# MLA and pooling encoder with a 32-expert layer: slot table from one-hot products on chip, and the held part of the weight stream changed

## What is computed

```
h = x + concat(attention(rms_norm(x)), pooling(rms_norm(x))) @ w_out
y = h + HierMoE(rms_norm(h, g_ffn))
HierMoE(a): gp = softmax(a @ w_group_router + b_group_router)     # 4 groups, the best one
            el = a @ w_expert_router + b_expert_router            # 8 experts per group, the best two
            y  = sum over the two experts of gate * (silu(a @ w_gate[e]) * (a @ w_up[e])) @ w_down[e]
```

## Time and profile before

| what | value |
|---|---|
| median of three runs | 644.66 us |
| profiled execution, its own time | 643.67 us |
| its span, first to last instruction | 642.0 us |
| TensorE busy | 530.8 us (83%) |
| VectorE / ScalarE / GpSimd busy | 223.6 / 147.0 / 133.2 us |
| mean DMA rate | 232 GB/s |

### The profile page before, as it was taken

How to read it: one execution, slowest core, us unless ns; L and a number is a source line. 1 busy time by engine, 2 the same in 40 slices (tenths; PEclk the granted TensorE clock), 3 DMA queues, 4 the chain that set the end, 5 groups by cost and what they waited for, 6 DMA issues and landing times.

```text
span 642.0 us, 8839 instructions
## 1 busy us (share of the span) xinstructions
PE 530.8 (83%) x3092; PEld 373.3 (58%) x3093; DVE 223.6 (35%) x602; ACT 147.0 (23%) x310; POOL 133.2 (21%) x200
## 2 busy tenths in 40 slices
PE   5889999997898989999725877989788897777762
PEld 4768988884444568888624545555445564434430
DVE  4743335225959562566650211121211211111110
ACT  6734343322546221121201101010100100000000
POOL 0122232032244000034323102111201232011110
PEclk9999999999999999999856989799989999889997
DMA  8730100000620039243467999999999999999992
GB/s 333 240 142 35 32 2 1 1 0 1 236 72 27 2 137 387 100 132 133 171 227 253 405 374 388 392 367 379 388 393 390 392 392 379 403 390 392 388 363 34
DMA packets 31163, 148.81 MB, mean 232 GB/s; under 512 B 7139, under 2 KB 7798, under 8 KB 18822
## 3 DMA queue, kind: packets, MB, share of 16 engines
q1 hardware_dynamic: 25376, 128.60, 50.2%
q0 software_dynamic: 5712, 19.72, 11.7%
q10 hardware_dynamic: 38, 0.01, 0.0%
HBM read 132.48 MB, written 17.00 MB: 233 GB/s over the span
## 4 chain that ended last, share of the span: by engine, by line
DMA 45%; PE 25%; issue 10%; DVE 6%; POOL 4%; ACT 1%; POOLq 0%; SPq 0%
DMA expert_w<-in_w_down 25%; DMA expert_w<-in_w_up 19%; PE ps L476 4%; PE ps L477 4%; PE ps L481 4%; PE ps L641 3%; POOL slot_tokens L1390 2%; PE ps L582 2%; DVE p_sb L1130 2%; PE ps L596 2%; PE ps L599 1%; PE ps L628 1%; PE ps L516 1%; DMA g_rows<-token_rows,idx_now 1%; PE ps L667 1%
## 5 line engine op out<-in xcount | busy, mean ns | idle before, releaser
L767 PE MATMUL ps<-expert_w,xT 128*64 128x256 f32 x1152 | 132.2, 386 | 16.4 <-DMA expert_w<-in_w_up 6.8
L767 PEld LDWEIGHTS ps<-expert_w,xT 128*64 128x64 f32 x1152 | 97.7, 140 | 55.5 <-issue 27.8
L783 PE MATMUL ps<-expert_w,hT 128*64 128x512 f32 x288 | 76.8, 681 | 23.7 <-DMA expert_w<-in_w_down 13.2
L1432 POOL DMA_INDIRECT out<-y_sb,idx_now x18 | 28.7, 1593 | 202.6 <-DVE y_sb L1302 201.8
L783 PEld LDWEIGHTS ps<-expert_w,hT 128*64 128x64 f32 x288 | 25.5, 155 | 63.1 <-issue 60.7
L1290 DVE SCALAR_TENSOR_TENSOR hid<-s_act,gate,ps 128x256 f32<-128x256 f32 x18 | 11.9, 660 | 141.5 <-ACT s_act L968 141.5
L476 PE MATMUL ps<-w_in_hi,aT_hi 128*128 128x384 f32 (+2 forms) x120 | 43.7, 368 | 0.0
L1302 DVE COPY y_sb<-ps 128x512 f32<-128x512 f32 x18 | 12.5, 692 | 89.5 <-PE ps L783 89.5
L477 PE MATMUL ps<-w_in_lo,aT_hi 128*128 128x384 f32 (+2 forms) x120 | 40.8, 344 | 0.0
L968 ACT ACTIVATE s_act<-ps 128x256 f32<-128x256 f32 x18 | 6.9, 384 | 133.7 <-PE ps L767 133.7
L973 ACT ACTIVATE y_sb<-ps 128x512 f32<-128x512 f32 x18 | 10.8, 597 | 105.6 <-PE ps L783 105.6
(11 more groups left out here) (205 smaller groups left out, 856.5 us busy)
## 6 DMA issues: line engine op xcount, KB each, us to landing
expert_w<-in_w_gate SPq DMA_DIRECT2D x32, 1024.0 KB, 9.7
expert_w<-in_w_up SPq DMA_DIRECT2D x32, 1024.0 KB, 8.5
expert_w<-in_w_down SPq DMA_DIRECT2D x32, 1024.0 KB, 10.4
w_in_raw<-in_w_in SPq DMA_DIRECT2D x8, 608.0 KB, 10.3
w_out_raw<-in_w_out SPq DMA_DIRECT2D x8, 512.0 KB, 3.6
token_rows<-rows SPq DMA_DIRECT2D x6, 528.0 KB, 3.4
out<-h_sb SPq DMA_DIRECT2D x6, 512.0 KB, 2.9
x_sb<-in_x_prompt SPq DMA_DIRECT2D x4, 512.0 KB, 9.9
```

Of the source, the lines that this page charges most:

```text
L767: mm = pe.matmul(ps[r, 2, g * FH:(g + 1) * FH], xT[:, q.o, k, r], w_gu(b, lane, k, g), start=(k == 0), stop=(k == KD - 1))
L783: mm = pe.matmul(ps[r, 4 + half, :], hT[:, q.o, k, r], w_dn(b, lane, k, half), start=(k == 0), stop=(k == 1))
L1432: pool.indirect_dma_start(out=out, out_offset=bass.IndirectOffsetOnAxis(ap=idx, axis=0), in_=y_sb[:, buf, :], in_offset=None, compute_op=A ...
```

## The change

The slot table of the first pass is no longer read back from HBM. VectorE compares the place of each token (rank within its lane, plus 64 for the second lane) with 0 to 127 and so makes a one-hot matrix `slot_a`; ScalarE scales the one-hot expert rows by the token number and by the gate (`slot_b`, 64 columns); TensorE sums the products of both choices of all six tiles in PSUM (`slots`). VectorE adds the number of the spare row and has `idx_all` and `gate_all` on chip. The table in HBM stays for further passes only. Spare rows no longer exist in `token_rows`: the gather has a bound of T - 1, and a slot with a larger index is left out of it. Gates have an HBM table of their own.

The router works on the transposed, unnormed h: the gain of the norm is multiplied into `w_router` at the start (it needs a new short transfer, `g_router`), and the reciprocal root mean square scales the logits. The last tile's normed row is made by ScalarE and GpSimd instead of VectorE. Only the two gate parts of pair 1 are loaded after the last h; four parts of pair 1 and all of pair 2 wait for the first gather.

```diff
+                (g_router[:, :], a["g_ffn_norm"][0].rearrange("(k p) -> p k", k=KD)),
...
-            sp.dma_start(table[T:T + P, :], a["zeros"]).then_inc(setup_dram, 16)
...
-                    load_pair(sp, 1, 1, range(3))
+                    load_pair(sp, 1, 1, range(2))
...
-            load_pair(sp, 1, 1, range(3, 4))
             store_rows(NT - 1)
-            sp.wait_ge(slots_stored, 2 * NT * 16)
+            store_gates(NT - 2)
+            store_gates(NT - 1)
+            sp.wait_ge(main.gathered[0], 16)
+            load_pair(sp, 1, 1, range(2, 6))
+            load_pair(sp, 2, 2)
             sp.wait_ge(counts_done, 1)
-            sp.dma_start(idx_all[:, 0:PAIRS], slot_table[0:BLOCK, :]...)
...
+            def slots(i):
+                pe.wait_ge(slot_a_done, i + 1)
+                pe.wait_ge(slot_b_done, 2 * (i + 1))
+                for c in range(2):
+                    mm = pe.matmul(ps[:, 5, 0:2 * E], slot_a[:, c, :], slot_b[:, c, :], start=(i == 0 and c == 0),
+                                   stop=(i == NT - 1 and c == 1))
...
             for i in range(NT):
-                out_half(i, 0)
+                out_part(i, 0, False)
                 if i >= 1:
-                    row_transposes(i - 1)
-                out_half(i, 1)
+                    h_transposes(i - 1, 1)
+                out_part(i, 0, True)
+                if i >= 1:
+                    logits(i - 1, 0)
+                    logits(i - 1, 1)
                 if i >= 2:
-                    ranks(i - 2)
+                    slots(i - 2)
+                out_part(i, 1, False)
+                h_transposes(i, 0)
+                out_part(i, 1, True)
                 if i >= 1:
-                    logits(i - 1)
+                    ranks(i - 1)
...
+            pool.wait_ge(idx_done, 3)
             pool.wait_ge(rows_stored, 16 * NT)
...
+            def gather(dst, src, idx, done):
+                pool.indirect_dma_start(out=dst, out_offset=None, in_=src, in_offset=bass.IndirectOffsetOnAxis(ap=idx, axis=0),
+                                        bounds_check=T - 1, oob_is_err=False).then_inc(done, 16)
```

More of the change, by code:

```diff
@@ L42 @@
 BLOCK = 2 * LANE * PAIRS
-ROW = D + E
 N_VEC = KD + KQ + KKV + 2 + NG
@@ L113, in region @@
             return got
-        (consts, bf_consts, gains, tok_ids, neg_half, idx_pos, counts_i, m_sum, w_router) = region(
-            4096,
+        (consts, bf_consts, gains, tok_ids, neg_half, idx_pos, counts_i, m_sum, w_router, g_router,
+         idx_all, idx_more, idx_now, gate_all, gate, gate_rows) = region(
+            4448,
             [("consts_sb", [P, C_W], F32), ("bf_consts", [P, 2, P], BF16), ("gains", [P, N_VEC], F32),
@@ new lines, in hT_out, with slot_gates @@
+            def hT_out(i, half):
+                act.wait_ge(a2_tr, 2 * i + half + 1)
+                if i >= 1:
+                    act.wait_ge(lg_mm, i)
+                act.activation(a2T[:, 4 * half:4 * half + 4, :], ps[:, 4, :].rearrange("p (k t) -> p k t", k=4),
+                               ACT.Copy).then_inc(a2T_done, 1)
+            def slot_gates(i):
+                act.wait_ge(wts_done, i + 1)
+                if i >= 1:
+                    act.wait_ge(slot_mm, i)
+                for c in range(2):
+                    ins = act.activation(slot_b[:, c, E:2 * E], route_f[:, 224 + E * c:224 + E * (c + 1)], ACT.Copy,
+                                         scale=route_f[:, 185 + c:186 + c])
+                ins.then_inc(slot_b_done, 1)
@@ L948, in _, with slot_values @@
+            def slot_values(i):
+                act.wait_ge(val_done, i + 1)
+                for c in range(2):
+                    ins = act.activation(slot_b[:, c, 0:E], route_f[:, 224 + E * c:224 + E * (c + 1)], ACT.Copy,
+                                         scale=route_f[:, 396 + c:397 + c])
+                ins.then_inc(slot_b_done, 1)
+            for i in range(NT):
+                square_h(i, 0)
                 if i >= 1:
                     route_exps(i - 1)
-                act.wait_ge(a2_tr, i + 1)
+                hT_out(i, 0)
@@ L1067, in _ @@
                     dve.wait_ge(tables_set, 4)
+                    dve.tensor_tensor(w_router[:, :, :], w_router[:, :, :],
+                                      g_router[:, :].unsqueeze(2).to_broadcast([P, KD, EG + E]), ALU.mult).then_inc(tables_set, 1)
                 if 1 <= i < NT - 1:
@@ L1230, in positions @@
                 dve.wait_ge(rank_mm, i + 1)
                 dve.wait_ge(mask_done, i + 1)
-                rank = ps[:, 6, 128:128 + E]
+                rank = ps[:, 6, 0:E]
+                for c in range(2):
+                    ins = dve.tensor_tensor_reduce(out=RF[:, 320 + E * c:320 + E * (c + 1)], in0=RF[:, 224 + E * c:224 + E * (c + 1)],
+                                                   in1=rank, scale=1.0, scalar=0.0, op0=ALU.mult, op1=ALU.add,
+                                                   accum_out=RF[:, 390 + c:391 + c])
@@ L1255, in _ @@
                     route_weights(i - 1)
-            positions(NT - 2)
+                residual(i, 1)
+                if i >= 1:
+                    slot_of(i - 1)
+                    table_place(i - 1)
+                    gate_row(i - 1)
+                if i + 1 < NT:
+                    second_norm(i)
             route(NT - 1)
-            positions(NT - 1)
             route_weights(NT - 1)
+            slot_of(NT - 1)
+            table_place(NT - 1)
+            dve.wait_ge(slot_mm, NT)
+            for lane in range(2):
+                r = slice(lane * LANE, (lane + 1) * LANE)
+                dve.tensor_scalar(idx_all[r, 0:PAIRS], ps[r, 5, PAIRS * lane:PAIRS * (lane + 1)], spare_row[r], None,
+                                  ALU.add).then_inc(idx_done, 1)
+            dve.tensor_copy(idx_all[:, PAIRS:], spare_row).then_inc(idx_done, 1)
+            for lane in range(2):
+                r = slice(lane * LANE, (lane + 1) * LANE)
+                dve.tensor_copy(gate_all[r, :], ps[r, 5, E + PAIRS * lane:E + PAIRS * (lane + 1)]).then_inc(idx_done, 1)
+            gate_row(NT - 1)
             dve.wait_ge(total_mm, 1)
@@ L1428, in gather_pair @@
                 ready((idx_set, count))
-                gather(g_rows[:, b, :], idx_now[:, b:b + 1], main.gathered[b])
+                gather(g_rows[:, b, :], table, idx_now[:, b:b + 1], main.gathered[b])
             def add_rows(q, n, buf, idx):
```

349 lines of the change are left out of this document (197 added, 152 removed).

## The result

The changed kernel takes 650.19 us (median of nine runs, 646.75 to 655.37) against 645.21 us before (nine runs, 643.77 to 646.30): a ratio of 1.0086, 95% interval 1.0053 to 1.0118. It is slower, where I had forecast 1.3% faster. Its runs also lie further apart, 8.6 us against 2.5.

What follows compares the result with a forecast made beforehand. The prediction took TensorE to bound the projection, small steps the routing and DMA bytes the stream. Start +4.3, projection +4.0, routing -12.9 and stream -4.0 gave -8.6, from 644.66 to 636.0 us, range 629 to 643.

Steps and rivals of the forecast that it cites:

- What bounds the kernel now: Opening step: TensorE bounds the output projection, small steps the 29.3 us of routing, and DMA bytes the stream after it.
- -4.0: Stream, gather's landing to last weights: two added parts +5.05, rows left out -8.8, shorter rows 0.2; range -8.7 to +4.9.
- The price of a row left out: Stream: 870 rows left out, 3.67 MB, worth 8.8 us at the weights' price of 2.41 us per MB.
- It ends 0.8 us before the index, so it costs nothing: Last tile's routing: row store in at 11.1 us after the last h, index columns ready at 11.85.
- the routing: Last h to gather's landing: from 29.2 to 16.3 us, -12.9, range -10 to -14.
- The rival with a late row store: Routing: row store through GpSimd ends at 15 to 17, behind two scatters and VectorE; 639 to 641 us; chance 0.08.
- The start: Up to TensorE's first k transposes: X - 0.7 = +4.3 us, range 0.7 to 10.
- X: Start: time of the 1,024 four-byte pieces of `g_router` ahead of the head gains; taken as 5 us, bounds 1 to 11.
- The projection: Output projection to the last h: added slot products, operand changes and waits on TensorE, +4.0 us, range 2 to 6.
- tile 1's term: Projection: tile 1's first transposes now wait for its x, which landed late behind pair 0's weights; 0.7 us.
- some 870 fewer: Sign to check: the software queue should carry some 870 packets fewer than before.
- Slower: Outcome, chance 0.11; its main rival, chance 0.14: left-out indices still move rows in the stream, 645 to 651 us.

Runs made afterwards that it cites:

- e1: Changed kernel with pair 1's weight parts loaded where they were before the change, two fewer behind the gather: 654.60 us, +1.29% to the kernel before.
- e5: Changed kernel with the last tile's two scatters ahead of the first two gathers in GpSimd's queue: 646.35 us, +0.35% to the kernel before.
- e6: Kernel before the change with only the bound added to its gathers: 641.18 us, -0.56% to the kernel before.
- e10: Changed kernel with e2, e4, e5, e9 and pair 0's weight parts spread behind the x loads: 638.35 us, -1.24% to the kernel before.
- e15: The kernel of e10 run again, unchanged: 638.25 us, -1.19% to the kernel before.
- e11: The kernel of e10 with the last row again made by ScalarE and GpSimd: 640.48 us, -1.04% to the kernel before.
- e9: Changed kernel with each tile's row store issued before the wait for the next tile's h: 648.57 us, +0.36% to the kernel before.
- r1: The changed kernel run again as it is, as base for the other runs: 650.36 us, +0.89% to the kernel before.
- e7: Changed kernel with the edits of e3, e4 and e5 together: 641.90 us, -0.41% to the kernel before.
- e3: Changed kernel with row stores of even and odd tiles counted by separate signals: 649.10 us, +0.50% to the kernel before.
- e16: Repeat run of e10 with the first gather ahead of the last tile's scatters: 639.37 us, -0.89% to the kernel before.
- e2: Changed kernel with the last tile's row made by VectorE instead of ScalarE and GpSimd: 651.98 us, +0.88% to the kernel before.
- e4: Changed kernel with `g_router` loaded last of the short transfers and router weights scaled one tile later: 646.31 us, +0.19% to the kernel before.

## Why the forecast was wrong, by its own steps

- **The step that failed is the one under "What bounds the kernel now": "from 342.7 to 626.3 us the DMA share is 1.01 and TensorE has 53 us to spare, so time there is bytes."** Over its first 30 us this holds only as long as pair 0's buffer comes free before the parts have run out. In the kernel before it did, just: 8.26 of the 8.39 MB were in at the refill. The change moved the readback of the second pass's indices behind the gathers and the last scatters; the refill came 6.2 us later, and the DMA engines waited. -4.0 became +2.6. e1 and e5 show it: two parts fewer gave nothing, an earlier readback gave 3.5 us and, in its profile, a stream of 280.7 where 279.6 was forecast.
- **The price of a row left out, 2.41 us per MB, is the second part of that miss.** I had counted the bytes rightly (3.67 MB, measured 3.67) and priced them like weights, -8.8. The bound alone gave 3.6 us (e6), and from the refill on, where the two queues' shares add up to 1.01, 3.36 MB gave 3.6 us. How the 6.6 us of the stream divide between the wait and the price is not settled, since e5 removes the wait and comes within 1.1 us of the forecast, but e10, e15 and e11, which remove it too, have streams of 280.9 to 285.5. The three numbers of rows in the forecast also add up to 880 and not to 870, which is 0.1 us.
- **"It ends 0.8 us before the index, so it costs nothing"**, of the row store: it ended 2 us behind the index. I had priced the store at its own 3.4 us, from the moment at which its row was ready, and overlooked the new wait for the store of tile 4 and the two weight parts in the same queue. e9, which removes both, gave 3.4 us by the ratios, of which its profile shows 1.1 to 1.8 at the landing. The index branch itself was 2.2 late, less than the 2.6 of the stall beside GpSimd, a thing that I had priced for the scatters and not for the multiplication. Together the routing gave -8.1 for -12.9. The rival with a late row store had a chance of 0.08 and its store ending at 15 to 17, where it did end; but it named two scatters and VectorE as the cause, not the queue, so that is luck.
- **The start, +4.3**, came to +2.5 (3.5 in r1). X is 2 to 3 where 5 was taken, inside its range. By the forecast's own X - 0.7 that is +1.3 to +2.3; the rest is the half clock behind a longer wait of TensorE, which was in no case of mine.
- **The projection, +4.0**, came to +4.4. A stage is 14.27 us (269.43 to 283.70 between first halves of h); 14.3 was forecast. Only tile 1's term (0.7) was tried by itself.
- **Packets: "some 870 fewer"** is wrong, though the bytes are right: 134 fewer in e6, and short ones take the place of most.
- **The tail**, +2.4: the last products run at a lower granted clock in this profile (5.37 us for 3.67). The kernel before with the bound alone (e6) has 5.37 too, so it is not the change's own. No experiment was aimed at it, and it varies between 16.2 and 19.4 us over the other profiles; open.

"Slower" had a chance of 0.11, and for a reason that did not come: a left-out index still moving its row.

e10 and e15 are at -8.0 and -7.6 us, close to the forecast's -8.6, but that does not confirm it. They also hold edits that the change has nothing to do with, such as tile 1's x and the order of the row stores, and these were not tried on the kernel before. With only waits of the change itself taken out (e7) it is -0.41%, 2.6 us, no better than the bound alone on the kernel before (e6, -0.56%).

## What to carry to other kernels

A DMA share of 1.0 over a long stretch says nothing of its first buffers: count the parts that may be loaded before the first buffer comes free, and compare that with the chain that frees it, further passes included. Bytes left out are not worth the price of other bytes until a run has shown it. When a small transfer is moved, price it where it now lies in its queue, not by the median of its kind: the same row store took 3.4 us by the median and 6.4 (e3) or 10.6 (322.77 to 333.4) behind weights, the same readback 5 (e10) or 10 (e16). And an order of issue alone was worth 3.4 us (e9, a store before the next wait) and 3.5 us (e5, a scatter before a gather), as much each as the bound on the gathers, 3.6 us.

## What the runs showed of the hardware

- A gather with a bound leaves the row's bytes out, and most of the rows left out still appear as a short packet: 3.67 MB fewer, 134 packets fewer and 737 more of under 512 bytes (e6).
- 1,142 packets of under 512 bytes went in 1.2 us, 1 ns each over all the engines together, against 9 in the earlier trace rows: short packets have no single price.
- A VectorE `tensor_scalar` of four columns took 2.87 us when it began 0.02 us after a GpSimd multiplication over 1,024 columns, and 2.86 to 2.88 in all ten profiles of kernels with that multiplication; in those without it (such as e2 and e10) no such step stands. The Trainium skill, SBUF — State Buffer, section Who interferes with whom, says that whichever of a VectorE instruction in a two-port mode (`tensor_scalar` is one that can be) and a GpSimd instruction issues first holds the shared ports, and the other "fully blocks". This case's trace agrees: 0.2 us of work ended with the 2.86 us multiplication.
- TensorE's clock was granted at 0.50 for 43.1 to 48.3 us behind 3.69 us of idle time, and at 1.00 in 41.8 to 47.1 us behind 1.57 us and in 40.9 to 45.4 us behind 0.98 us (e4). In e7 it was 0.60 in 257.9 to 262.0 us behind 2.19 us. The lower level cost the 16 products 1.9 us, 1.1 of it on the path.
